# Three dealt schedules in an attention block, and every second scaling of the probabilities on ScalarE

## The chip, the cores and the metric

The kernel runs on one core of one Trainium2 chip. The metric is the time of one execution on the device in microseconds, and its profile is of one such execution.

## The reference

One layer of a hybrid encoder block on x of 1024 tokens by 1024 channels, all in float32:

```
h = RMSNorm(x);  proj = h @ w_in
A: 4 heads, two score maps each; softmax of each, p0 - lam * p1, times v (128 wide)
B: 8 heads of 64, own chunk of 64 and 8 chunks before it, bias by relative place
C: 8 heads of 64, causal, score + c_q - c_k (cumulative log forget)
x += (sum_i sigmoid(gate_i) * (o_i @ w_br_i)) @ w_out
x += (silu(RMSNorm(x) @ w_gate) * (RMSNorm(x) @ w_up)) @ w_down;  out = RMSNorm(x)
```

## The kernel before, in words

Every product is done in three passes of TensorE on a high and a low part of each operand (`three_passes`, L183 to L185). The kernel has four blocks: norm, attention, merge, feed-forward. Only the attention block is touched. It begins near 80 us and ends near 829 us.

**Units.** The attention block goes through 12 units, four for each branch: units 0 to 3 are A (one head of two maps), 4 to 7 B (two heads), 8 to 11 C (two heads). A unit has 16 steps, s = 0 to 15: a step is one tile of 128 queries of one map or head against its keys. The number of key tiles n grows with s, to 8 in A and C and to 5 in B. In B and C steps 0 to 15 have n = 1, 2, 1, 2, 3, 4, 3, 4 and then 5, 5, ... (B) or 5, 6, 5, 6, 7, 8, 7, 8 (C).

**One step's way through the engines**, with the short names used below:
- S(s): TensorE, scores of step s into PSUM (`score`, L930, L931; in C also the causal mask, L933).
- READ(s): VectorE adds the bias, takes the row's extreme and writes to SBUF (`read_scores`, L781); in C it also makes the shift (L790).
- exp(s): ScalarE, in place, with the row sum (`exp`, L652).
- SCALE(s), in B and C: VectorE takes the reciprocal of the row sum (L812) and multiplies the row by it in place (`scale_probs`, L814). In A it is MIX(i) for two steps at once: reciprocal, ratio, and p0 - lam * p1 (`mix_maps`, L822 to L827).
- T(s): TensorE transposes the row by tiles into the turn banks 4 and 5 (`turn_probs`, L959); in A only for odd s. A row of more than 4 tiles takes two chunks, and a chunk has to wait until the bank of the chunk two before it has been read.
- CHhi(s), CHlo(s): ScalarE copies a chunk out (L665, L667), then VectorE makes its low part (L799, L802).
- V(g): TensorE multiplies by v, once for every two steps (`times_v_a` L975, L977; `times_v_bc` L993, L994); then o_low on ScalarE (L676, L684) and o_out on VectorE (L838, L848). V(g) waits for o_out(g-1).

**Projection in between.** TensorE also projects k, q and v of the next unit: 24 pieces of 6 matmuls, in 6 groups of 4. Four pieces stand ahead of the steps, and `PIECES_AT[s]` says how many follow T(s). `EVAC_AT` says in which step a group is taken out of PSUM: `project_out` on ScalarE (L627 to L633) and, for groups 0 to 3, `project_low` on VectorE (two instructions of one group, L743 to L752). `SPLIT_AT` says in which step ScalarE makes the high part of the next weight slab (`split_hi`, L618, called SPLIT below); GpSimd then makes the low part (L591, POOL split). A group may start once the group before it in the same PSUM bank is out (`PROJ_BANKS`); groups 1, 3, 4 and 5 share bank 6. Unit 11 has nothing after it but two groups of a gate, and a list of its own, `LAST_PIECES_AT`.

**Order.** Each engine has its own instruction stream, written as a loop over s, and all of them run in order. In iteration s, which goes from 0 to 17, the order before is:
- TensorE: S(s+2), T(s), pieces, and V(s/2-1) when s is even.
- ScalarE: project_out, CHhi(s), exp(s+2), SPLIT, and o_low when s is odd.
- VectorE, A: MIX (s even), project_low, READ(s+2), CHlo(s), o_out (s odd). B and C: project_low, READ(s+2), SCALE(s+1), CHlo(s), o_out (s odd).

Of the kernel before, what the change touches and what calls it, by code (L numbers as in the profile page):

```python
# [32 lines left out]
P = 128  # L33
# [81 lines left out]

PIECES_AT = [2, 2, 2, 2, 1, 1, 1, 1, 0, 1, 1, 1, 1, 1, 1, 2, 0]
EVAC_AT = {0: 0, 2: 1, 4: 2, 8: 3, 13: 4, 16: 5}
SPLIT_AT = {0: 1, 4: 2, 8: 3}
PROJ_BANKS = (3, 6, 1, 6, 6, 6)
LAST_PIECES_AT = [0, 1, 0, 1, 0, 1, 0, 1, 0, 1, 0, 1, 0, 1, 1, 0, 0]  # L120
LAST_EVAC_AT = {8: 0, 16: 1}
assert sum(LAST_PIECES_AT) == 2 * GROUP_PIECES
assert PIECES_BEFORE + sum(PIECES_AT) == 6 * GROUP_PIECES

# [293 lines left out]
def block_attention(nc, ps, keep, scratch, w_in_k, w_br_b):  # L418
    h_hi, h_lo, ident = keep["h_hi"], keep["h_lo"], keep["ident_r"][:, :].bitcast(F32)
    with ExitStack() as ctx:  # L420
# [35 lines left out]
        probs_ready, rinv_ready, ratio_ready, mixed = sem("probs_ready"), sem("rinv_ready"), sem("ratio_ready"), sem("maps_mixed")  # L456
        scaled = sem("probs_scaled")
        turned, turned_hi, turned_out = sem("chunk_turned"), sem("chunk_hi"), sem("chunk_out")
# [155 lines left out]
        def _(act):  # L614
# [30 lines left out]
            def exp(b, c, s):  # L645
# [3 lines left out]
                else:  # L649
# [4 lines left out]
                                     accum_out=rowsum[:, s % 4:s % 4 + 1]).then_inc(probs_ready, 1)  # L654

            def chunks_hi(b, c, s):
                done, tile = chunks_through(b, s - 1), 0
                i, m = place_of(b, s)
                for j, size in enumerate(chunks_of(b, i)):
                    lc = done + j  # L660
                    act.wait_ge(turned, c["banks"] + (V_CHUNKS + lc + 1))
                    if b == 0:
                        if lc >= 4:
                            act.wait_ge(pv_chunk, c["chunks"] + (lc - 3))
                        nc.scalar.activation(pta_hi[:, lc % 4, 0:size * P], turn_bank[lc % 2][:, 0:size * P], ACT.Copy).then_inc(turned_hi, 1)  # L665
                    else:
                        nc.scalar.activation(turned_place(ptb_hi, b, i, m, tile, size),  # L667
                                             turn_bank[lc % 2][:, 0:size * P].rearrange("p (t q) -> p t q", q=P),
                                             ACT.Copy).then_inc(turned_hi, 1)
                    tile += size  # L670
# [15 lines left out]
            def unit_body(b, it, du, last=False):  # L686
# [5 lines left out]
                for lc in range(V_CHUNKS):  # L692
                    v_hi(b, c, lc, du)
                for s in range(STEPS + 2):
                    if last and s in LAST_EVAC_AT:
                        project_out(UNITS, LAST_EVAC_AT[s], 0)
                    elif not last and s in EVAC_AT:
                        project_out(c["unit"] + 1, EVAC_AT[s], 1 - du)
                    if s in turns:
                        chunks_hi(b, c, s)  # L700
                    if s + 2 < STEPS:
                        exp(b, c, s + 2)
                    if last and s == 3:
                        act.wait_ge(w_loaded[1], 8 * LAST_SLAB + 24)
                        nc.scalar.activation(w_hi[:, 1, 0:BR_K, :], w_raw[:, 1, 0:BR_K, :], ACT.Copy).then_inc(w_hi_done, 1)
                    if not last and s in SPLIT_AT:
                        j = SPLIT_AT[s]
                        odd = 3 * (du + 1) + j
                        act.wait_ge(proj_ready, 2 * (slab + (j - 1)))
                        split_hi(slab + j, odd % 2, 6 * b + 3 * it + odd // 2)  # L710
                    if b == 0 and s >= 3 and s % 2 == 1:
                        o_low_a(c, (s - 3) // 2)
                    if b > 0 and s >= 3 and s % 2 == 1:
                        o_low_bc(c, (s - 3) // 2)

# [20 lines left out]
        def _(dve):  # L736
# [71 lines left out]
            def scale_probs(b, c, s):  # L808
# [3 lines left out]
                nc.vector.reciprocal(rinv[:, s % 4:s % 4 + 1], rowsum[:, s % 4:s % 4 + 1]).then_inc(rinv_ready, 1)  # L812
                dve.wait_ge(rinv_ready, UPB * UNIT_OUTS + turns)
                nc.vector.tensor_scalar(row, row, rinv[:, s % 4:s % 4 + 1], None, ALU.mult).then_inc(scaled, 1)  # L814

# [35 lines left out]
            def unit_body(b, it, du, project=True):  # L851
# [12 lines left out]
                if b > 0:  # L864
                    scale_probs(b, c, 0)
                for s in range(STEPS + 2):
                    if b == 0 and s % 2 == 0 and s < STEPS:
                        mix_maps(c, s // 2)
                    if project and s in EVAC_AT:
                        project_low(c["unit"] + 1, EVAC_AT[s], 1 - du)  # L870
                    if s + 2 < STEPS:
                        read_scores(b, c, s + 2)
                    if b > 0 and s + 1 < STEPS:
                        scale_probs(b, c, s + 1)
                    if s in turns:
                        chunks_low(b, c, s)
                    if b == 0 and s >= 3 and s % 2 == 1:
                        o_out_a(c, (s - 3) // 2)
                    if b > 0 and s >= 3 and s % 2 == 1:
                        o_out_bc(c, (s - 3) // 2)  # L880

# [14 lines left out]
        def _(pe):  # L896
# [48 lines left out]
            def turn_probs(b, c, s):  # L945
# [5 lines left out]
                else:  # L951
                    pe.wait_ge(scaled, STEPS * (c["unit"] - UPB) + (s + 1))
                    src = probs_of(b, s)
# [43 lines left out]
            def unit_body(b, it, du, last=False):  # L997
                c = counts(b, it, du) | {"par": du}
                turns = turns_of(b)
                pieces_at = LAST_PIECES_AT if last else PIECES_AT  # L1000

# [848 lines left out]
```

## Time and profile before

| | us |
|---|---|
| median of 3 runs | 2068.73 (2067.91 to 2071.92) |
| the profiled execution | 2067.87 |
| its span, first to last instruction | 2066.1 |
| TensorE busy | 1962.2 |
| VectorE, ScalarE, GpSimd busy | 1030.5, 703.9, 95.0 |
| mean granted TensorE clock | 0.992 |

The three other blocks keep TensorE almost without a gap; the attention block takes about 36% of the span and has nearly all the gaps that are left. One unit of A takes 60.3 us, one of B 61.4 us, one of C 68.8 us. A time behind the name of an engine is what it is busy; a time in square brackets behind an instruction is how long its engine stood idle ahead of it, with the instruction that released it.

### The profile page before, as it was taken

To read this page: it belongs to the slowest core of one execution; us is meant where nothing else is said; L and a number is where in the kernel's file an instruction comes from. 1 tells how busy PE (TensorE), PEld (TensorE's weight loads), DVE (VectorE), ACT (ScalarE), POOL (GpSimd) and SP (SyncE) were. 2 spreads that over 40 slices of the span, in tenths; PEclk is the share of its full clock that TensorE was granted. 3 is DMA by queue.
4 is the path that set the end of the run, shared out by engine and by line. 5 is a ranking of instruction groups with operands and counts; after the bars stand their busy time and mean duration, and the time that the engine had idled before them with its cause. 6 is when DMAs were issued, how large, how long until landed. Compare 5 with 4: busy or idle time off the path is not lost. (4 is left out here: it accounts for less than half of the span.)

```text
span 2066.1 us, 26269 instructions
## 1 busy us (share of the span) xinstructions
PE 1962.2 (95%) x9542; PEld 1629.9 (79%) x9542; DVE 1030.5 (50%) x1950; ACT 703.9 (34%) x1310; POOL 95.0 (5%) x59
## 2 busy tenths in 40 slices
PE   6999999999999998999999999999999999999997
PEld 3777778878778777788787878788888888888886
DVE  4466666666777787324433237623343334323326
ACT  5355555555555555221431112421112101121122
POOL 1111111110110000000000000000000000000000
PEclk9999999999999999999999999999999999999998
DMA  7422222212222110412111123120121101211112
GB/s 227 124 62 64 69 74 64 65 50 75 51 82 72 42 47 31 123 46 82 51 46 46 46 89 111 30 68 25 51 61 52 49 30 51 61 51 41 41 51 82
DMA packets 145268, 133.32 MB, mean 65 GB/s; under 512 B 7476, under 2 KB 130484, under 8 KB 142888
## 3 DMA queue, kind: packets, MB, share of 16 engines
q1 hardware_dynamic: 141768, 132.16, 21.6%
q8 instruction: 44, 0.72, 0.1%
q10 hardware_dynamic: 3424, 0.17, 0.1%
q14 instruction: 32, 0.26, 0.0%
HBM read 109.17 MB, written 16.06 MB: 61 GB/s over the span
## 5 line engine op out<-in xcount | busy, mean ns | idle before, releaser
L183 PE MATMUL ps<-h_hi,w_hi 128*128 128x512 f32 x1664 | 667.1, 401 | 13.5 <-DVE w_lo L1223 4.7
L185 PE MATMUL ps<-h_hi,w_lo 128*128 128x512 f32 x1664 | 651.7, 392 | 0.0
L184 PE MATMUL ps<-h_lo,w_hi 128*128 128x512 f32 x1664 | 651.3, 391 | 0.0
L183 PEld LDWEIGHTS ps<-h_hi,w_hi 128*128 128x128 f32 x1664 | 314.2, 189 | 77.4 <-DVE w_lo L1223 4.8
L185 PEld LDWEIGHTS ps<-h_hi,w_lo 128*128 128x128 f32 x1664 | 313.7, 189 | 67.4
L184 PEld LDWEIGHTS ps<-h_lo,w_hi 128*128 128x128 f32 x1664 | 314.6, 189 | 59.0
L1598 DVE TENSOR_TENSOR residual<-residual,ps 128x512 f32<-128x512 f32 x240 | 162.7, 686 | 113.7 <-PE ps L185 109.0
L1589 DVE TENSOR_TENSOR w_lo<-w_raw,w_hi 128x1024 fp32r<-128x1024 f32 x46 | 56.4, 1226 | 158.5 <-ACT w_hi L1491 158.5
L1499 ACT ACTIVATE bias<-ps 128x512 f32<-128x512 f32 x44 | 26.1, 594 | 311.5 <-PE ps L185 311.5
L184 PE MATMUL ps<-w_down_lo,act_hi 128*128 128x512 f32 x320 | 124.6, 389 | 0.0
L185 PE MATMUL ps<-w_down_hi,act_lo 128*128 128x512 f32 x320 | 124.6, 389 | 0.0
L183 PE MATMUL ps<-w_down_hi,act_hi 128*128 128x512 f32 x320 | 124.6, 389 | 0.0
L959 PE MATMUL ps<-ident_r,probs_bc 128*128 128x128 f32 x528 | 82.5, 280 | 37.4 <-DVE probs_tb_lo L802 26.1
L667 ACT ACTIVATE probs_tb_hi<-ps 128x384 fp32r<-128x384 f32 (+2 forms) x192 | 81.8, 461 | 103.2 <-PE ps L959 102.5
L591 POOL TENSOR_TENSOR w_lo<-w_raw,w_hi 128x1024 fp32r<-128x1024 f32 (+1 forms) x36 | 85.7, 2381 | 634.3 <-ACT w_hi L618 594.1
L1607 DVE TENSOR_TENSOR bias<-ps,bias 128x512 f32<-128x512 f32 x44 | 30.4, 692 | 167.2 <-PE ps L185 167.2
L781 DVE CUSTOM_DVE_ANT_0 probs_bc<-ps,bias 128x640 f32<-128x640 f32 (+7 forms) x128 | 90.2, 705 | 41.8 <-PE ps L931 15.8
L802 DVE TENSOR_TENSOR probs_tb_lo<-ps,probs_tb_hi 128x384 fp32r<-128x384 f32 (+2 forms) x192 | 93.9, 517 | 17.6 <-ACT probs_tb_hi L667 17.3
L959 PEld LDWEIGHTS ps<-ident_r,probs_bc 128*128 128x128 f32 x528 | 58.7, 141 | 53.1 <-DVE probs_bc L814 29.4
L814 DVE TENSOR_SCALAR probs_bc<-probs_bc,rinv 128x640 f32<-128x640 f32 (+7 forms) x128 | 95.2, 744 | 4.6
L930 PE MATMUL ps<-k_stack,q_stack 128*128 128x320 f32 (+5 forms) x288 | 97.0, 341 | 0.0
L1504 ACT ACTIVATE act_hi<-bias 128x512 fp32r<-128x512 f32 x44 | 27.8, 632 | 202.9 <-DVE bias L1607 202.9
(202 smaller groups left out, 2740.8 us busy)
## 6 DMA issues: line engine op xcount, KB each, us to landing
w_raw<-in_w_in SPq DMA_DIRECT2D x60, 512.0 KB, 3.8
w_raw<-in_w_gate_up SPq DMA_DIRECT2D x44, 512.0 KB, 3.8
k_stack<-k_stack SPq DMA_DIRECT2D x24, 512.0 KB, 6.3
w_raw<-in_w_down SPq DMA_DIRECT2D x22, 512.0 KB, 3.5
x_all<-in_x SPq DMA_DIRECT2D x8, 512.0 KB, 8.6
bias<-bias_a_scratch SPq DMA_DIRECT2D x4, 1024.0 KB, 6.0
heads_bc_scratch<-heads_out SPq DMA_DIRECT2D x8, 512.0 KB, 2.9
bias<-neg_c_scratch SPq DMA_DIRECT2D x4, 1024.0 KB, 5.1
```

The lines of the kernel that those rows point to most:

```text
L183: nc.tensor.matmul(out, w_hi, x_hi, start=first, stop=False)
L184: nc.tensor.matmul(out, w_hi, x_lo, start=False, stop=False)
L185: return nc.tensor.matmul(out, w_lo, x_hi, start=False, stop=last)
L591: nc.gpsimd.tensor_tensor(w_lo[part], w_raw[part], w_hi[part].bitcast(F32), ALU.subtract).then_inc(w_split, 1)
L667: nc.scalar.activation(turned_place(ptb_hi, b, i, m, tile, size), turn_bank[lc % 2][:, 0:size * P].rearrange("p (t q) -> p t q", q=P), ACT ...
L781: nc.vector.tensor_tensor_reduce(out=row_view(probs_of(b, s)[:, 0:n * P], n), in0=scores_view(s, n), in1=row_view(window, n), scale=-1.0, ...
L802: nc.vector.tensor_tensor(turned_place(ptb_lo, b, i, m, tile, size), turn_bank[lc % 2][:, 0:size * P].rearrange("p (t q) -> p t q", q=P), ...
L814: nc.vector.tensor_scalar(row, row, rinv[:, s % 4:s % 4 + 1], None, ALU.mult).then_inc(scaled, 1)
L930: nc.tensor.matmul(dst, q, k_st[:, par, 2 * m, keys], start=True, stop=False)
L959: last = nc.tensor.transpose(turn_bank[lc % 2][:, x * P:(x + 1) * P], src[:, tile * P:(tile + 1) * P], ident[:, :])
L1589: nc.vector.tensor_tensor(w_lo[kind], w_raw[:, raw, :], w_hi[kind].bitcast(F32), ALU.subtract).then_inc(w_split, 1)
L1598: nc.vector.tensor_tensor(res[:, t, cols], res[:, t, cols], bank(ps, 4 + o % 4), ALU.add).then_inc(added, 1)
```

## The change

Four things, all in the attention block:
1. `PIECES_AT`, `EVAC_AT` and `SPLIT_AT` get a list for each branch. The number of pieces for a unit is the same. A moves one piece from step 9 to 10; B and C are dealt anew, in the late steps mostly two in an odd iteration and none in an even one. Evacuations move with the groups; SPLITs move to iterations 0, 2, 10 (A), 0, 3, 12 (B), and stay at 0, 4, 8 in C.
2. In B and C the multiplication of SCALE(s) for even s goes to ScalarE as an activation (Copy with a scale from SBUF, `scale_probs` of ScalarE). The reciprocal stays on VectorE for all s.
3. ScalarE's order in an iteration becomes: project_out, SPLIT, o_low, CHhi(s), the scaling of s+1 (s odd), exp(s+2).
4. VectorE's order in A becomes: READ(s+2), MIX, CHlo(s), project_low, o_out. B and C keep theirs.

```diff
+PIECES_AT = [
+    [2, 2, 2, 2, 1, 1, 1, 1, 0, 0, 2, 1, 1, 1, 1, 2, 0],
+    [3, 2, 1, 1, 1, 2, 0, 1, 1, 2, 0, 1, 1, 2, 0, 2, 0],
+    [2, 1, 2, 2, 1, 2, 2, 1, 1, 1, 0, 1, 0, 2, 0, 2, 0],
+]
+EVAC_AT = [
+    {0: 0, 2: 1, 4: 2, 8: 3, 13: 4, 16: 5},
+    {1: 0, 2: 1, 5: 2, 9: 3, 13: 4, 16: 5},
+    {1: 0, 3: 1, 5: 2, 7: 3, 12: 4, 16: 5},
+]
+SPLIT_AT = [{0: 1, 2: 2, 10: 3}, {0: 1, 3: 2, 12: 3}, {0: 1, 4: 2, 8: 3}]
...
-        scaled = sem("probs_scaled")
+        scaled = [sem("probs_scaled_even"), sem("probs_scaled_odd")]
...
+            def scale_probs(b, c, s):
+                row = probs_of(b, s)[:, 0:tiles_of(b, place_of(b, s)[0])[1] * P]
+                act.wait_ge(rinv_ready, UPB * UNIT_OUTS + STEPS * (c["unit"] - UPB) + (s + 1))
+                nc.scalar.activation(row, row, ACT.Copy, scale=rinv[:, s % 4:s % 4 + 1]).then_inc(scaled[0], 1)
...
+                if b > 0:
+                    scale_probs(b, c, 0)
                 for s in range(STEPS + 2):
...
-                    if s in turns:
-                        chunks_hi(b, c, s)
-                    if s + 2 < STEPS:
-                        exp(b, c, s + 2)
...
-                    if b == 0 and s >= 3 and s % 2 == 1:
-                        o_low_a(c, (s - 3) // 2)
-                    if b > 0 and s >= 3 and s % 2 == 1:
-                        o_low_bc(c, (s - 3) // 2)
+                    if s >= 3 and s % 2 == 1:
+                        if b == 0:
+                            o_low_a(c, (s - 3) // 2)
+                        else:
+                            o_low_bc(c, (s - 3) // 2)
+                    if s in turns:
+                        chunks_hi(b, c, s)
+                    if b > 0 and s % 2 == 1 and s + 1 < STEPS:
+                        scale_probs(b, c, s + 1)
+                    if s + 2 < STEPS:
+                        exp(b, c, s + 2)
...
-                dve.wait_ge(rinv_ready, UPB * UNIT_OUTS + turns)
-                nc.vector.tensor_scalar(row, row, rinv[:, s % 4:s % 4 + 1], None, ALU.mult).then_inc(scaled, 1)
+                if s % 2 == 1:
+                    dve.wait_ge(rinv_ready, UPB * UNIT_OUTS + turns)
+                    nc.vector.tensor_scalar(row, row, rinv[:, s % 4:s % 4 + 1], None, ALU.mult).then_inc(scaled[1], 1)
...
+                    if b > 0 and project and s in EVAC_AT[b]:
+                        project_low(c["unit"] + 1, EVAC_AT[b][s], 1 - du)
+                    if s + 2 < STEPS:
+                        read_scores(b, c, s + 2)
                     if b == 0 and s % 2 == 0 and s < STEPS:
                         mix_maps(c, s // 2)
-                    if project and s in EVAC_AT:
-                        project_low(c["unit"] + 1, EVAC_AT[s], 1 - du)
-                    if s + 2 < STEPS:
-                        read_scores(b, c, s + 2)
                     if b > 0 and s + 1 < STEPS:
                         scale_probs(b, c, s + 1)
                     if s in turns:
                         chunks_low(b, c, s)
...
+                    if b == 0 and s in EVAC_AT[b]:
+                        project_low(c["unit"] + 1, EVAC_AT[b][s], 1 - du)
...
-                    pe.wait_ge(scaled, STEPS * (c["unit"] - UPB) + (s + 1))
+                    pe.wait_ge(scaled[s % 2], STEPS // 2 * (c["unit"] - UPB) + (s // 2 + 1))
```

## Rows read from the trace of the kernel before

**Rows 1.** The page, part 1: busy time and share of the span.
```profile
PE 1962.2 (95%) x9542; PEld 1629.9 (79%) x9542; DVE 1030.5 (50%) x1950; ACT 703.9 (34%) x1310; POOL 95.0 (5%) x59
```
**Rows 2.** Stretches: length, then busy us (and instructions) by engine, clock, DMA.
```profile
85.47:145.75 60.28, 56.63 (x309) 47.95 (x308) 37.94 (x86) 30.02 (x67) 7.34 (x4) 1.00 0.21 52
326.54:387.94 61.40, 57.60 (x333) 49.36 (x332) 43.08 (x106) 34.28 (x79) 7.77 (x5) 1.00 0.24 65
641.74:710.51 68.77, 62.97 (x369) 54.23 (x368) 52.71 (x122) 37.10 (x79) 7.17 (x3) 1.00 0.22 62
776.76:830.00 53.24, 42.99 (x268) 36.79 (x267) 41.49 (x115) 30.18 (x69) 1.27 (x1) 0.97 0.08 30
744.00:748.00 4.00, 1.92 (x13) 1.66 (x12) 3.86 (x12) 2.78 (x7) 0.71 (x1) 0.97 0.00 0
748.00:752.00 4.00, 4.00 (x16) 3.44 (x16) 3.90 (x6) 1.77 (x5) 1.68 (x1) 0.60 0.27 57
```
**Rows 3.** Groups of instructions by shape, 325 to 822 us: busy, mean ns, idle before.
```profile
L959 PE MATMUL ps<-ident_r,probs_bc 128*128 128x128 f32 x520 | 81.5, 280 | 37.4 <-DVE probs_tb_lo L802 26.1 <-DVE probs_bc L814 11.1
...
L814 DVE TENSOR_SCALAR probs_bc<-probs_bc,rinv 128x128 f32<-128x128 f32 x16 | 18.6, 1160 | 0.6
...
L652 ACT ACTIVATE probs_bc<-probs_bc,neg_max 128x640 f32<-128x640 f32 x32 | 26.6, 831 | 6.9 <-DVE neg_max L781 6.8
...
L652 ACT ACTIVATE probs_bc<-probs_bc,shift 128x1024 f32<-128x1024 f32 x8 | 9.2, 1153 | 1.6 <-DVE shift L790 1.4
...
L652 ACT ACTIVATE probs_bc<-probs_bc,shift 128x128 f32<-128x128 f32 x8 | 3.2, 401 | 8.1 <-DVE shift L790 8.1
...
L705 ACT ACTIVATE w_hi<-w_raw 128x512 fp32r<-128x512 f32 x1 | 0.6, 615 | 0.0
```
**Rows 4.** Instructions in order of time, unit 2 (branch A): start us, us, engine.
```profile
214.00 2.39 POOL L591 TENSOR_TENSOR w_lo<-w_raw,w_hi 128x1024 fp32r<-128x1024 f32 x1 [31.69 <-ACT w_hi L618]
...
215.19 1.48 DVE L827 SCALAR_TENSOR_TENSOR probs_a<-probs_a,ratio 128x256 f32<-128x256 f32 x1
...
233.56 0.35 ACT L676 ACTIVATE o_low<-ps,rinv 128x128 f32<-128x128 f32 x1
...
234.43 0.38 PE L975 MATMUL ps<-v_split,probs_ta_hi 128*128 128x256 f32 x1 [0.78 <-DVE heads_out L838]
...
234.72 0.89 DVE L827 SCALAR_TENSOR_TENSOR probs_a<-probs_a,ratio 128x640 f32<-128x640 f32 x1
...
236.33 0.69 DVE L752 SCALAR_TENSOR_TENSOR q_stack<-ps,q_stack 64x512 fp32r<-64x512 f32 x1
237.05 0.96 DVE L781 CUSTOM_DVE_ANT_0 probs_a<-ps,bias 128x768 f32<-128x768 f32 x1
...
242.51 0.38 PE L975 MATMUL ps<-v_split,probs_ta_hi 128*128 128x256 f32 x1 [1.61 <-DVE heads_out L838]
```
**Rows 5.** In order of time, unit 4 (branch B), iterations 9 and 10.
```profile
357.50 0.31 PE L930 MATMUL ps<-k_stack,q_stack 128*128 128x320 f32 x1
357.65 0.31 PE L931 MATMUL ps<-k_stack,q_stack 128*128 128x320 f32 x1
...
359.75 0.77 PE L959 MATMUL ps<-ident_r,probs_bc 128*128 128x128 f32 x5 [1.79 <-DVE probs_tb_lo L802]
...
360.61 2.39 POOL L591 TENSOR_TENSOR w_lo<-w_raw,w_hi 128x1024 fp32r<-128x1024 f32 x1 [9.41 <-ACT w_hi L618]
...
360.88 2.48 DVE L814 TENSOR_SCALAR probs_bc<-probs_bc,rinv 128x640 f32<-128x640 f32 x1
...
363.87 0.77 PE L959 MATMUL ps<-ident_r,probs_bc 128*128 128x128 f32 x5 [1.39 <-DVE probs_tb_lo L802]
...
365.58 0.55 DVE L814 TENSOR_SCALAR probs_bc<-probs_bc,rinv 128x640 f32<-128x640 f32 x1
```
**Rows 6.** In order of time, unit 8 (branch C), iterations 5 and 6.
```profile
664.45 2.35 DVE L814 TENSOR_SCALAR probs_bc<-probs_bc,rinv 128x384 f32<-128x384 f32 x1
...
666.85 0.55 PE L959 MATMUL ps<-ident_r,probs_bc 128*128 128x128 f32 x3 [1.13 <-DVE probs_bc L814]
```

More of the change, by code:

```diff
@@ L114 @@
 PIECES_BEFORE_V = 2
-PIECES_AT = [2, 2, 2, 2, 1, 1, 1, 1, 0, 1, 1, 1, 1, 1, 1, 2, 0]
-EVAC_AT = {0: 0, 2: 1, 4: 2, 8: 3, 13: 4, 16: 5}
-SPLIT_AT = {0: 1, 4: 2, 8: 3}
+PIECES_AT = [
[3 rows of a table added]
+]
+EVAC_AT = [
[3 rows of a table added]
+]
+SPLIT_AT = [{0: 1, 2: 2, 10: 3}, {0: 1, 3: 2, 12: 3}, {0: 1, 4: 2, 8: 3}]
 PROJ_BANKS = (3, 6, 1, 6, 6, 6)
@@ L122 @@
 assert sum(LAST_PIECES_AT) == 2 * GROUP_PIECES
-assert PIECES_BEFORE + sum(PIECES_AT) == 6 * GROUP_PIECES
+assert all(PIECES_BEFORE + sum(pieces) == 6 * GROUP_PIECES for pieces in PIECES_AT)
 def counts(b, it, du):
@@ L696, in unit_body @@
                         project_out(UNITS, LAST_EVAC_AT[s], 0)
-                    elif not last and s in EVAC_AT:
-                        project_out(c["unit"] + 1, EVAC_AT[s], 1 - du)
-                    if s in turns:
-                        chunks_hi(b, c, s)
-                    if s + 2 < STEPS:
-                        exp(b, c, s + 2)
+                    elif not last and s in EVAC_AT[b]:
+                        project_out(c["unit"] + 1, EVAC_AT[b][s], 1 - du)
                     if last and s == 3:
@@ L705, in unit_body @@
                         nc.scalar.activation(w_hi[:, 1, 0:BR_K, :], w_raw[:, 1, 0:BR_K, :], ACT.Copy).then_inc(w_hi_done, 1)
-                    if not last and s in SPLIT_AT:
-                        j = SPLIT_AT[s]
+                    if not last and s in SPLIT_AT[b]:
+                        j = SPLIT_AT[b][s]
                         odd = 3 * (du + 1) + j
@@ L876, in unit_body @@
                         chunks_low(b, c, s)
[L877 to L880, printed above, removed]
+                    if b == 0 and s in EVAC_AT[b]:
+                        project_low(c["unit"] + 1, EVAC_AT[b][s], 1 - du)
+                    if s >= 3 and s % 2 == 1:
+                        if b == 0:
+                            o_out_a(c, (s - 3) // 2)
+                        else:
+                            o_out_bc(c, (s - 3) // 2)
             for g in range(4):
@@ L999, in unit_body @@
                 turns = turns_of(b)
-                pieces_at = LAST_PIECES_AT if last else PIECES_AT
+                pieces_at = LAST_PIECES_AT if last else PIECES_AT[b]
                 done = [0]
```

## The prediction

> **What bounds the kernel now.** The page first: TensorE is busy 95% of the span [rows 1], so only its gaps, its clock and its work can give time, and the change leaves its work as it is. Then the stretches, to see where the gaps lie. One unit of A has 60.28 - 56.63 = 3.65 us of gaps, one of B 3.80, one of C 5.80, and the last unit with its end 10.25 [rows 2]. VectorE is busy 63%, 70% and 77% of these units, ScalarE 50 to 56%: neither is full, so the gaps are moments in which one of them comes late. Then the groups: TensorE's transposes T wait 37.4 us in B and C, 26.1 for CHlo and 11.1 for SCALE, both on VectorE [rows 3]. Last the instructions in order of time, to see why VectorE was late. Three causes come back in every unit:
> - In A, V waits 0.78 and 1.61 us for o_out, which waits for an o_low that stands behind CHhi and exp on ScalarE [rows 4]. Both follow an iteration in which ScalarE had waited for a READ that stood behind MIX and project_low.
> - In B and C, two project_low instructions of 0.69 us each stand ahead of READ and CHlo in iteration 8; T(9) waits 1.79 us for CHlo in B [rows 5].
> - A SCALE of 640 columns takes 0.55 us, but 2.48 us beside a POOL split of 2.39 us, and T(10) behind it waits 1.39 us [rows 5]. In C a SCALE of 384 takes 2.35 us, and T(6) waits 1.13 us [rows 6]. The mean of the 128-column form, 1160 ns, is such a mixture [rows 3].
>
> What a gap costs is a little more than its idle time: matmuls of 320 columns start 0.15 us apart and show as 0.31 us [rows 5], so about 0.16 us is hidden at each. With five to seven stops a unit the losses are about 4.4 us (A), 4.7 (B), 7.0 (C). C loses clock too: behind the stretch with TensorE busy 1.92 of 4 us the granted clock is 0.60 for 4 us, a mixture of 1.2 and 2.4 GHz, and costs 4 x 0.4 = 1.6 us [rows 2].
>
> **The scaling moved.** For B and C, 8 units, 64 scalings go from VectorE to ScalarE. ScalarE has no such operation yet. From below, a plain copy takes 0.615 us for 512 columns; from above, exp takes 0.401, 0.831 and 1.153 us for 128, 640 and 1024 [rows 3]. I take exp, since it also reads a value per partition, and drop its sum read-out: 0.40, 0.62, 0.83 and 1.04 us for 1, 3, 5 and 7 tiles, by its line. That is 5.4 us in a unit of B, 5.8 in C, 44.6 in all; 0.1 us less for each by the copy, 38. VectorE loses, at its free speed (0.55 us for 640 columns, so about 0.47 on the mean of these sizes, an estimate), some 30 us. Worth more: the long SCALEs are those of steps 2 and 10 (B) and 2, 6, 10 (C), all even, so this class of waits leaves VectorE: some 2 us each, 17 of them, 33 us. Not all was on the path: that of step 2 made TensorE wait for nothing.
>
> The page of the Trainium skill "Perfetto Trace Analysis", section "Optimizing Scalar/DVE Operations", speaks against the move: where VectorE has its faster mode it is the quicker engine, and work should leave it only when it is full. It is not full here [rows 2]. By that rule the 64 moves add 44.6 - 30 = 14.6 us of work; were all of it on the path, the 40 us summed below would be 25, and the time 2044. It is a form of the first rival below.
>
> Where is ScalarE's new work hidden? It stands in odd iterations ahead of exp(s+2). Late in B and C those now mostly hold two pieces (2 x 1.4 us), so from T(s) to T(s+1) there are 3.8 us, in which CHhi (about 0.8), the scaling 0.83 and exp 0.83 + 0.19 fit. exp(s+2) comes some 0.8 us later; behind it stand CHhi(s+1) and SCALE(s+2), with an even iteration's V to cover them. In C at iterations 10 to 12, with 0, 1 and 0 pieces, VectorE's and TensorE's work are level (3.4 against 3.1 us in iteration 12); I count 0.4 us there. If this cover is gone, each scaling costs up to its own length.
>
> **The deal of pieces and evacuations, B and C.** I followed the queues with the durations above. B: group 3 ends in iteration 8, is taken out in 9, and the next piece stands in 9: one project_out (about 0.6 us, as the copy of 512 columns [rows 3]), two project_low of 0.69 [rows 4] and the semaphores between end 2.55 us after the group, while V, S and T cover 2.1: 0.45 us. C: the same in iteration 7, 0.2, and T(8) behind it 0.3. The SPLIT ahead of exp at iteration 4 of C lets the POOL split start before SCALE(5): blocked 2 us, of which T(5) sees 0.4. Iteration 0 of both meets SCALE(1) in the same way, hidden behind three pieces in B, 0.1 us in C. In B SPLIT in 3 and 12 misses the scalings. New waits: B 0.6, with 0.6 more for what I didn't find, C 1.4. Kept of the loss: B 4.7 - 1.2 = 3.5 gained, 14 for four units (unit 6 has one wait more); C 7.0 - 1.4 = 5.6 for three units, 17, with the clock loss of unit 9 within it.
>
> **A.** READ ahead of MIX and project_low lets exp start 1 to 2 us sooner, o_low is first in its iteration, SPLIT moves to iteration 2 where ScalarE waits anyway. All of 4.4 us would go. Two waits come. In iterations 8 and 9 there are no pieces: from S(10), READ(10) starts after 1.07 us, takes 0.9 to the next start, reciprocal and ratio 0.42 and MIX(4) 0.89 [rows 4], 3.3 us in all, while S, V and S take TensorE 2.5: T(9) waits 0.8. SPLIT at 10 ends about 7.9 us after S(10), and MIX(5) wants to start at 8.2: a MIX beside a POOL split was stretched to 1.48 us, to the split's end [rows 4], so T(11) comes 1.4 us late. Should MIX start first, this is nothing. 4.4 - 2.2 = 2.2 us a unit, 9 for four; 3.6 a unit at best.
>
> The SPLIT in A, B and C moves ahead of CHhi and exp by at most 1.1 us, and the DMA of the slab after it moves with it; the slab is needed only many pieces later, and no TensorE wait for a load shows in the attention block. Reordering o_low costs CHhi 0.36 us, covered as above.
>
> **Unit 11** keeps its list. It lives from VectorE, 78% busy [rows 2], and ScalarE's added 5.8 us is in the same chain as VectorE's 3.9 less. I take nothing, from +3 to -3.
>
> **Sum.** 9 + 14 + 17 + 0 = 40 us of the profiled 2067.87. The followed queues hold only the waits I looked for; I take off 0.5 us for each of the 11 full units: 34.5. The median shown is 0.9 above the profiled one. 2068.7 - 34.5 = 2034.
>
> **Rivals.**
> - *The waits move* (0.17): T waits for the scaling on ScalarE or for MIX beside the split in most units, and half the 40 us comes back. For it: the evacuations fit by tenths of a microsecond, and ScalarE's copies of T's output come within each iteration. Against it: the free time of both engines [rows 2]. About 2049.
> - *ScalarE becomes the late link* (0.09), the other side: each scaling delays exp(s+2), that READ's successor and the next odd SCALE by its full length, and no piece covers it. Then 44.6 us stand against 40: 2073. It decides from 0.63 us exposed at each of the 64. Against it: ScalarE is 54% busy in C, about 65% after.
> - *Nothing* (0.06): the relief and the added work cancel, 2068.
> - *All gaps go* (0.13), with no MIX beside the split and no clock loss: A 3.6 x 4, B 4.2 x 4, C 6.8 x 3 with unit 11 giving 3: 54 us, 2015.
> - The forecast has 0.55, its own range 2024 to 2044.
>
> **Numbers.** 0.2% is 4 us, about what a measurement here can tell. Faster: 0.55 + 0.17 + 0.13 and a little of the rest, 0.87; same 0.05; slower 0.08. The range goes from the best case to beyond half the gain: 2014 to 2056.
>
> **What would show it.** L814 x64 with no form near 1160 ns; 64 new ScalarE copies of 0.4 to 1.05 us; V's 0.78 and 1.61 us waits in A gone; a wait of T for MIX in iterations 9 and 11 of A; units of about 58, 58 and 63 us; clock 1.00 from 740 to 760 us. I am wrong if T's wait is for the new ScalarE copies by over 0.6 us a time, or if A's units don't shorten.

## The result, and the profile after

The changed kernel takes 2018.38 us (2015.51 to 2020.33, 4 runs), the kernel before 2068.77: ratio 0.9753, 95% interval 0.9736 to 0.9769. That is 50.4 us faster; 34.5 were forecast. The time lies in the stated range of 2014 to 2056, but outside the 2024 to 2044 of the forecast itself; it is nearest to the rival *all gaps go* (2015, chance 0.13). The profiled execution is the fastest of the four: 2015.51 us, with a span of 2013.7 against 2066.1. Below, times of stretches are of that execution. Line numbers differ after the change: S is L952 and L953, READ L799, exp L660, MIX L846, VectorE's SCALE L833, ScalarE's scaling L667, T L981, CHhi L678 and L680, V L997 and L1015, SPLIT L626, POOL split L599, o_low L689 and L697, o_out L857 and L867.

The page, part 1, to be read beside [rows 1]:

```profile
PE 1947.1 (97%) x9542; PEld 1626.9 (81%) x9542; DVE 982.1 (49%) x1886; ACT 747.6 (37%) x1374; POOL 95.4 (5%) x59
```

The number of matmuls is the same. VectorE has 64 instructions fewer and is busy 48 us less, ScalarE has 64 more and is busy 44 us more.

Stretches of one unit of A, B, C, and of the last unit to beyond its end, as in [rows 2]:

```profile
144.31:202.07 57.76, 55.52 (x310) 47.91 (x309) 38.00 (x86) 32.85 (x68) 7.41 (x4) 1.00 0.26 73
317.59:374.18 56.59, 56.56 (x334) 49.50 (x332) 37.23 (x98) 38.98 (x87) 7.84 (x5) 1.00 0.26 70
545.04:607.49 62.45, 61.92 (x369) 54.28 (x368) 45.99 (x114) 41.98 (x87) 7.19 (x3) 1.00 0.24 69
729.57:780.00 50.43, 40.14 (x268) 35.66 (x267) 38.12 (x108) 36.01 (x80) 1.29 (x1) 1.00 0.13 46
```

The gaps of TensorE went from 3.65 to 2.24 us in A, from 3.80 to 0.03 in B, from 5.80 to 0.53 in C. By unit starts (the first transpose of v): A 10.0 us shorter in four units, B 19.0, the first three units of C 19.3, the last unit to the end of its last o_out 5.2 (52.6 to 47.4, with its clock at 1.00 where it was 0.97), together 53.5. What stands ahead of unit 0 is 1.1 us longer, which makes the 52.4 of the spans; its code is the same, and its length goes from 85.3 to 87.8 us in the traces below. The section on the time before says that the attention block has nearly all the gaps: by the trace of before it has 56.6 of 103.9 us. The rest, 16.8 us ahead of the block and 30.5 behind it, the change doesn't touch. Where the clock had fallen in the middle of C, it now holds:

```profile
740.00:760.00 20.00, 19.70 (x131) 17.73 (x130) 18.76 (x53) 17.19 (x38) 0.61 (x1) 1.00 0.00 1
```

Groups by shape, 317 to 780 us, as in [rows 3]:

```profile
L981 PE MATMUL ps<-ident_r,probs_bc 128*128 128x128 f32 x528 | 80.7, 276 | 6.6 <-ACT probs_bc L667 5.3 <-DVE probs_bc L833 1.1 <-DVE probs_tb_lo L820 0.2
...
L667 ACT ACTIVATE probs_bc<-probs_bc,rinv 128x640 f32<-128x640 f32 x24 | 20.0, 832 | 4.7 <-DVE rinv L830 4.4
L833 DVE TENSOR_SCALAR probs_bc<-probs_bc,rinv 128x256 f32<-128x256 f32 x16 | 15.7, 981 | 0.6
...
L667 ACT ACTIVATE probs_bc<-probs_bc,rinv 128x384 f32<-128x384 f32 x16 | 9.9, 617 | 9.2 <-DVE rinv L830 9.1
...
L667 ACT ACTIVATE probs_bc<-probs_bc,rinv 128x896 f32<-128x896 f32 x8 | 8.4, 1045 | 2.1 <-DVE rinv L830 1.7
...
L667 ACT ACTIVATE probs_bc<-probs_bc,rinv 128x128 f32<-128x128 f32 x16 | 6.4, 403 | 11.9 <-DVE rinv L830 11.4
```

T waited 37.4 us, and now 6.6. The copy on ScalarE costs what exp costs in [rows 3] (832 ns for 640 columns against 831). And the blocked SCALEs (held up by a POOL split on GpSimd) aren't gone: the mean of the 256-column form is 981 ns, where an unblocked one took 353. 17 SCALEs took over 1 us before, 9 do now.

Unit 2 (A) in order of time, the two waits that were forecast to come:

```profile
231.39 0.76 PE L981 MATMUL ps<-ident_r,probs_a 128*128 128x128 f32 x5 [0.90 <-DVE probs_a L846]
...
235.92 2.39 POOL L599 TENSOR_TENSOR w_lo<-w_raw,w_hi 128x1024 fp32r<-128x1024 f32 x1 [19.13 <-ACT w_hi L626]
...
236.24 2.88 DVE L846 SCALAR_TENSOR_TENSOR probs_a<-probs_a,ratio 128x768 f32<-128x768 f32 x1
...
239.18 0.87 PE L981 MATMUL ps<-ident_r,probs_a 128*128 128x128 f32 x6 [1.34 <-DVE probs_a L846]
```

Unit 8 (C), iteration 4, a SCALE of an odd step that the POOL split holds up, as SCALE(6) was in [rows 6]. TensorE waits 0.20 us for it, where it waited 1.13 for SCALE(6):

```profile
562.23 2.39 POOL L599 TENSOR_TENSOR w_lo<-w_raw,w_hi 128x1024 fp32r<-128x1024 f32 x1 [10.64 <-ACT w_hi L626]
...
563.07 1.84 DVE L833 TENSOR_SCALAR probs_bc<-probs_bc,rinv 128x512 f32<-128x512 f32 x1
...
564.96 0.66 PE L981 MATMUL ps<-ident_r,probs_bc 128*128 128x128 f32 x4 [0.20 <-DVE probs_bc L833]
```

### The profile page after: what moved, and what is told of

The parts are those of the page before. It is cut to its first block and busy times, and to the rows that moved or that the text cites. A ratio compares the mean times of both kernels' runs of the same rounds, so it can differ in the third digit from the quotient of the medians.

```text
span 2013.7 us, 26237 instructions
## 1 busy us (share of the span) xinstructions
PE 1947.1 (97%) x9542; PEld 1626.9 (81%) x9542; DVE 982.1 (49%) x1886; ACT 747.6 (37%) x1374; POOL 95.4 (5%) x59
## 5 line engine op out<-in xcount | busy, mean ns | idle before, releaser
L191 PEld LDWEIGHTS ps<-h_hi,w_hi 128*128 128x128 f32 x1664 | 313.8, 189 | 73.3 <-DVE w_lo L1245 4.8
L799 DVE CUSTOM_DVE_ANT_0 probs_bc<-ps,bias 128x640 f32<-128x640 f32 (+7 forms) x128 | 90.4, 707 | 55.8 <-PE ps L953 28.2
L599 POOL TENSOR_TENSOR w_lo<-w_raw,w_hi 128x1024 fp32r<-128x1024 f32 (+1 forms) x36 | 86.1, 2392 | 582.2 <-ACT w_hi L626 522.9
L820 DVE TENSOR_TENSOR probs_tb_lo<-ps,probs_tb_hi 128x384 fp32r<-128x384 f32 (+2 forms) x192 | 93.5, 514 | 15.7 <-ACT probs_tb_hi L680 14.9
L680 ACT ACTIVATE probs_tb_hi<-ps 128x384 fp32r<-128x384 f32 (+2 forms) x192 | 81.9, 461 | 47.3 <-PE ps L981 45.1
L952 PE MATMUL ps<-k_stack,q_stack 128*128 128x320 f32 (+5 forms) x288 | 96.8, 340 | 0.0
L953 PE MATMUL ps<-k_stack,q_stack 128*128 128x320 f32 (+5 forms) x288 | 94.7, 332 | 0.0
L1211 ACT ACTIVATE gate_sigmoid<-ps 128x512 f32<-128x512 f32 x46 | 27.4, 598 | 169.3 <-PE ps L193 169.2
L981 PE MATMUL ps<-ident_r,probs_bc 128*128 128x128 f32 x528 | 80.7, 276 | 6.6 <-ACT probs_bc L667 5.3
```

The costliest lines, as they stand in the source:

```text
L191: nc.tensor.matmul(out, w_hi, x_hi, start=first, stop=False)
L599: nc.gpsimd.tensor_tensor(w_lo[part], w_raw[part], w_hi[part].bitcast(F32), ALU.subtract).then_inc(w_split, 1)
L799: nc.vector.tensor_tensor_reduce(out=row_view(probs_of(b, s)[:, 0:n * P], n), in0=scores_view(s, n), in1=row_view(window, n), scale=-1.0, ...
L820: nc.vector.tensor_tensor(turned_place(ptb_lo, b, i, m, tile, size), turn_bank[lc % 2][:, 0:size * P].rearrange("p (t q) -> p t q", q=P), ...
L952: nc.tensor.matmul(dst, q, k_st[:, par, 2 * m, keys], start=True, stop=False)
L953: last_one = nc.tensor.matmul(dst, q, k_st[:, par, 2 * m + 1, keys], start=False, stop=not diagonal)
```

## The experiments

The change has three parts: the lists, the orders (ScalarE's, and VectorE's in A), and the scaling on ScalarE. Six kernels take the combinations that the two traces leave open; the other six vary one thing in the changed kernel or go on from it. Where an edit is long, the fence tells it in words.

### The orders alone

```diff
 # the kernel before, and:
+ ScalarE: project_out, SPLIT, o_low, CHhi(s), exp(s+2)
+ VectorE, A: READ(s+2), MIX, CHlo(s), project_low, o_out
```

> The kernel before with only the new orders of ScalarE and of VectorE in A; old lists, every scaling on VectorE. My theory (three causes of their own: order, lists, blocked scalings): A falls from 60.3 to about 58.0 us a unit, since its two waits for o_out go; B and C keep the blocked SCALEs and the late evacuation and give at most 1 us a unit. In all 10 to 14 us, about 2057. Rival (the moved scaling gives nearly everything in B and C and the order nothing outside A): the same A, B and C unchanged, 2059. Second rival (the order alone does it): B near 58, C near 65, about 2030.

Measured: 2084.18 us, ratio 1.0072 (1.0056 to 1.0089): slower by less than a percent, but clear of the noise. A did more than was expected, 60.3 to 57.1 us a unit. B and C got much longer, which no theory had. The second unit of each:

```profile
380.50:447.64 67.14, 59.78 (x333) 51.82 (x332) 43.47 (x102) 33.48 (x75) 7.49 (x5) 0.95 0.21 58
653.86:725.51 71.65, 63.94 (x369) 55.47 (x368) 51.51 (x122) 37.78 (x79) 7.06 (x3) 0.98 0.20 59
```

Unit 5 (B), iterations 8 and 9, in order of time. L632 and L633 are project_out, L755 and L758 project_low, L618 SPLIT, L591 the POOL split, L787 READ, L820 SCALE, L808 CHlo, L968 T:

```profile
413.20 0.59 ACT L633 ACTIVATE q_stack<-ps 64x512 fp32r<-64x512 f32 x1
...
413.81 1.06 ACT L618 ACTIVATE w_hi<-w_raw 128x1024 fp32r<-128x1024 f32 x1
...
414.05 0.69 DVE L758 SCALAR_TENSOR_TENSOR q_stack<-ps,q_stack 64x512 fp32r<-64x512 f32 x1
...
414.90 0.77 ACT L672 ACTIVATE probs_tb_hi<-ps 128x384 fp32r<-128x384 f32 x2
...
415.02 2.35 POOL L591 TENSOR_TENSOR w_lo<-w_raw,w_hi 128x1024 fp32r<-128x1024 f32 x1 [10.53 <-ACT w_hi L618]
...
415.72 2.00 DVE L820 TENSOR_SCALAR probs_bc<-probs_bc,rinv 128x640 f32<-128x640 f32 x1
...
417.64 0.87 DVE L808 TENSOR_TENSOR probs_tb_lo<-ps,probs_tb_hi 128x384 fp32r<-128x384 f32 x2
...
418.24 1.12 PE L968 MATMUL ps<-ident_r,probs_bc 128*128 128x128 f32 x4 [3.07 <-DVE probs_tb_lo L808]
```

In the old lists groups 2 and 3 are evacuated in iterations 4 and 8, and SPLITs 2 and 3 stand in the same two. With SPLIT ahead of CHhi and exp, the copy of T's output stands behind 1.2 us of project_out and 1.06 of SPLIT, the POOL split starts while VectorE still works off project_low and READ, and SCALE(9) then meets it. T(9) pays for all of it, for iteration 8 has no piece. T(5) waits 2.20 us for SCALE(5) in the same way, and T(1) 1.79 us for SCALE(1). These stops are not all of the loss: the unit is 5.7 us longer than one of before, its gaps are 3.6 us longer, and its matmuls are busy 2.2 us longer at a granted clock of 0.95.

### The moved scaling alone

```diff
 # the kernel before, and for even s in B and C:
+ ScalarE: project_out, CHhi(s), Copy(s+1) by rinv (s odd), exp(s+2), SPLIT, o_low
```

> The kernel before with only the scalings of even steps on ScalarE, ahead of exp(s+2); old lists, old orders. My theory: the waits behind a SCALE beside a POOL split go (1.4 us in B, 1.1 and 1.0 in C), the waits for the late evacuation stay: B 61.4 to about 59.5, C 68.8 to about 66, A unchanged; about 2051. Rival (the moved scaling gives nearly all of B and C): B 57, C 63, about 2030. Rival of the other side (ScalarE late without the new order): B and C longer than before.

Measured: 2067.15 us, ratio 0.9991 (0.9981 to 1.0001): nothing to be told. B 60.2, C 66.5 (a second one 68.1), the last unit 56.3 against 52.6. Not one SCALE of VectorE took over 1 us, so the cause was removed as meant. B and C gave 1.2 and 2.3 us a unit where the clock held. In units 6 and 9 it was 0.97 for 1.00 before; unit 6 was 0.6 us longer than before, and unit 9 only 0.7 shorter. V waits for o_out in B (0.75 us a unit) and C (1.01), and in the last unit at six places; four of them:

```profile
784.46 0.38 PE L1005 MATMUL ps<-probs_tb_hi,v_split 128*128 128x256 f32 x1 [1.40 <-DVE heads_out L859]
...
789.50 0.39 PE L1005 MATMUL ps<-probs_tb_hi,v_split 128*128 128x256 f32 x1 [0.63 <-DVE heads_out L859]
...
795.62 0.38 PE L1005 MATMUL ps<-probs_tb_hi,v_split 128*128 128x256 f32 x1 [1.01 <-DVE heads_out L859]
...
809.64 0.39 PE L1005 MATMUL ps<-probs_tb_hi,v_split 128*128 128x256 f32 x1 [0.94 <-DVE heads_out L859]
```

o_low stands behind the scaling and exp in the old order, and V behind o_low. Here "Perfetto Trace Analysis" of the Trainium skill, in "Optimizing Scalar/DVE Operations", would have been right: VectorE was not full, and the work taken from it bought nothing.

### The lists alone

```diff
 # the kernel before, with PIECES_AT, EVAC_AT and SPLIT_AT of the changed kernel
```

> The kernel before with only the lists for each branch; old orders, every scaling on VectorE. My theory: evacuation of group 3 one step later in B and earlier in C, two pieces in odd iterations: B about 59, C about 66.5, A unchanged or longer by the SPLIT at 10 that meets MIX(5); about 2050. Rival (lists matter only with the rest): within 5 us of before, since SCALEs are still blocked by the splits at their new places.

Measured: 2037.12 us, ratio 0.9852 (0.9832 to 0.9872), 31.6 us of the 50. One unit of each branch:

```profile
144.67:204.07 59.40, 56.34 (x310) 47.99 (x308) 37.96 (x86) 31.39 (x68) 7.39 (x4) 1.00 0.26 71
322.81:380.94 58.13, 57.20 (x334) 49.49 (x333) 40.09 (x106) 34.55 (x79) 7.58 (x5) 1.00 0.25 68
556.54:620.23 63.69, 62.70 (x370) 54.27 (x368) 47.98 (x122) 37.34 (x79) 7.21 (x3) 1.00 0.23 67
```

My theory had B and C right in kind and about 1 and 3 us too long, and A, which was to stay or to get longer, is 0.9 us shorter. The rival (within 5 us of before) fell. T(9)'s wait for the late evacuation in B, 1.79 us before, is 1.80 with the scaling alone and 3.07 with the orders alone; here it is gone, so it was the lists that took it away. Its row with the scaling alone:

```profile
360.57 0.77 PE L971 MATMUL ps<-ident_r,probs_bc 128*128 128x128 f32 x5 [1.80 <-DVE probs_tb_lo L812]
```

The SCALEs over 1 us fell from 17, of up to 2.48 us, to 7 of at most 1.51, with every scaling still on VectorE. In C the SPLITs keep their iterations, so there the pieces and the evacuations alone give 5.1 us a unit.

### The whole without the moved scaling

```diff
 # the changed kernel, and for even s too:
+ VectorE: tensor_scalar(row, row, rinv, mult); no scaling on ScalarE
```

> The changed kernel with every scaling back on VectorE (lists and orders new). It prices the move of the scaling within the whole. My theory: A stays at 57.8; in B the splits at 3 and 12 start just where no VectorE scaling is due or one that started before, so B loses about 1 us (57.6); C meets two blocked SCALEs and has VectorE and TensorE level late, so it loses 2 to 3 us (65): in all 12 to 15 us over the changed kernel, about 2031. Rival (the Trainium skill, Perfetto Trace Analysis: an engine that is not full should keep what it does faster): the same time or faster than the changed kernel, 2010 to 2018.

Measured: 2030.54 us, ratio 0.982 (0.98 to 0.984). Within the whole the moved scaling is worth 12.2 us: 1.5 a unit in B, 0.8 in C, 5.0 in the last unit (52.3 against 47.4 to its last o_out; the clock there was 0.94 against 1.00, about 3 us of it). The total came out as my theory had it, by other parts: B lost 1.5 for the 1 expected, C 0.8 for 2 to 3, and the last unit, of which nothing was said, the rest. The rival (an engine that is not full keeps its work) falls: what held for the scaling alone doesn't hold within the whole.

### The whole without the lists, and without the orders

```diff
 # first: the changed kernel with the lists of before
 # second: the changed kernel with the two orders of before
```

> The changed kernel with the lists of before (orders new, even scalings on ScalarE). With the orders alone B went from 61.4 to 66.6 and C to 72, and every blocked SCALE was that of steps 1, 5 and 9, which are odd and stay on VectorE here. Theory (the new orders put SPLIT ahead of exp, so that the POOL split starts just before the odd SCALE, and the new lists are what takes the splits away from it in B and covers it in C): B stays near 65, C near 70, A at 57.1 as with the orders alone; about 2068. Rival (the moved scaling frees enough of VectorE to make up for it): B near 60, C near 66, about 2035.

> The changed kernel with the orders of before (lists new, even scalings on ScalarE). Lists alone gave A 59.4, B 58.1, C 63.7. Theory (moving the scaling pays only where o_low does not stand behind it): A 59.4, B 57.5, C 63.5, and the last unit longer by its waits of V for o_out, as with the moved scaling alone; about 2036, no better than the lists alone. Rival (each part pays what it pays, whatever the others are): the scaling gives its 12 us on top of the lists, about 2025.

Measured: 2093.5 us, ratio 1.0112 (1.0097 to 1.0128), and 2057.55, ratio 0.9938 (0.9922 to 0.9953). Without the lists B is at 68.2, C at 73.3 and 71.8: slower than expected, and slower than the orders alone. Without the orders B is at 60.1, C at 65.6: the moved scaling makes the lists' kernel 20.4 us slower. The theory for that run expected 2036, no better than the lists alone; a loss of 20 us it had not foreseen. TensorE's waits in the last unit of the second (us in total, times, longest):

```profile
PE ps L1013 <- DVE heads_out L867: 6.6, 6, 1.9
PE ps L979 <- ACT probs_bc L667: 3.8, 2, 3.3
```

All eight, medians in us, then from the traces a unit of A, the second unit of B, the first of C, and the last unit to the end of its last o_out:

| lists | orders | scaling | whole kernel | A | B | C | last unit |
|---|---|---|---|---|---|---|---|
| - | - | - | 2068.8 | 60.3 | 61.4 | 68.8 | 52.6 |
| - | - | new | 2067.2 | 60.3 | 60.2 | 66.5 | 56.3 |
| - | new | - | 2084.2 | 57.1 | 67.1 | 72.9 | 52.3 |
| - | new | new | 2093.5 | 57.1 | 68.2 | 73.3 | 49.9 |
| new | - | - | 2037.1 | 59.4 | 58.1 | 63.7 | 53.6 |
| new | - | new | 2057.6 | 59.4 | 60.1 | 65.6 | 56.0 |
| new | new | - | 2030.5 | 57.8 | 58.1 | 63.2 | 52.3 |
| new | new | new | 2018.4 | 57.8 | 56.6 | 62.5 | 47.4 |

The lists of the branches don't reach the last unit, so its code is the same in pairs of these kernels, and the pairs show what the granted clock does: 52.6 and 53.6 us without the two other parts (clock 0.97 and 0.94), 49.9 and 47.4 with both (0.93 and 1.00). At a clock of 0.93 to 0.94 the last unit takes 53.6 us with neither, 56.0 to 56.3 with the scaling alone, 52.3 with the orders alone and 49.9 with both. Its rows in the kernels with the lists alone, with orders and scaling, and in a kernel further below that has the last unit of the changed one:

```profile
744.79:798.34 53.55, 44.13 (x268) 37.90 (x267) 41.42 (x115) 30.24 (x69) 1.27 (x1) 0.94 0.09 30
804.13:854.01 49.88, 42.74 (x268) 37.88 (x267) 37.61 (x107) 34.40 (x77) 1.30 (x1) 0.93 0.09 33
729.84:780.13 50.29, 43.08 (x268) 38.19 (x267) 37.59 (x107) 34.43 (x77) 1.30 (x1) 0.93 0.09 32
```

So the changed kernel's 47.4 us is that of an execution in which the clock held: the same code with the same gaps of 7.22 us took 50.3 in another, and the profiled execution is 2.9 us faster than the median.

### The other parity

```diff
 # the changed kernel, in B and C:
- ScalarE scales s+1 for s odd, VectorE the odd steps
+ ScalarE scales s+1 for s even, VectorE the even steps
```

> The changed kernel, but ScalarE scales the odd steps (in even iterations) and VectorE the even ones. Theory A (the POOL split meets the odd SCALE of steps 1 and 5, and the even iterations of ScalarE have no o_low): the blocked SCALEs go altogether and the time is the same or a little better, 2012 to 2020. Theory B (cover counts, which the two pieces of the odd iterations give to the even steps alone): T of odd steps follows at 2.5 us on the T before it, and waits for ScalarE's copy of 0.83 us: B and C 2 to 4 us a unit longer, 2030 to 2045.

Measured: 2032.8 us, ratio 0.982 (0.9805 to 0.9835). Both theories were half right. C is better, 62.1 us without any wait. B is worse, 59.6, but not for want of cover on ScalarE: the blocked SCALE is now an even one, in iteration 3, whose SPLIT goes with one piece. With a further wait of 0.75 us of a piece for project_low it makes the 2.4 us of gaps of a unit of B.

```profile
331.67 2.37 POOL L599 TENSOR_TENSOR w_lo<-w_raw,w_hi 128x1024 fp32r<-128x1024 f32 x1 [9.31 <-ACT w_hi L626]
...
331.83 2.43 DVE L831 TENSOR_SCALAR probs_bc<-probs_bc,rinv 128x384 f32<-128x384 f32 x1
...
334.39 0.54 PE L979 MATMUL ps<-ident_r,probs_bc 128*128 128x128 f32 x3 [1.63 <-DVE probs_bc L831]
```

### A mended

```diff
-SPLIT_AT = [{0: 1, 2: 2, 10: 3}, ...
+SPLIT_AT = [{0: 1, 2: 2, 11: 3}, ...
...
+                    if b == 0 and s == 8:
+                        mix_maps(c, s // 2)
                     if s + 2 < STEPS:
                         read_scores(b, c, s + 2)
-                    if b == 0 and s % 2 == 0 and s < STEPS:
+                    if b == 0 and s % 2 == 0 and s < STEPS and s != 8:
                         mix_maps(c, s // 2)
```

> The changed kernel with two edits in A: SPLIT 3 in iteration 11 and not 10, so that the POOL split does not meet MIX(5), and MIX ahead of READ in iteration 8 alone. Theory (the two waits of T for MIX, 0.90 and 1.34 us in each unit of A, come from these two): both go, 57.8 to 55.4 us a unit, 9 to 10 us in all, about 2008. Rival (the time comes back as a wait for o_out or for the evacuation of group 3, since READ(10) is later): less than 4 us gained.

Measured: 2008.12 us, ratio 0.9712 (0.9695 to 0.973). A unit of A takes 55.5 us, and both waits are gone. Of the rival's new wait 0.24 us a unit came (a piece for project_low). The MIX of 768 columns is back at 1.02 us, for it now starts before SPLIT does:

```profile
230.80 1.02 DVE L846 SCALAR_TENSOR_TENSOR probs_a<-probs_a,ratio 128x768 f32<-128x768 f32 x1
...
231.46 1.04 ACT L626 ACTIVATE w_hi<-w_raw 128x1024 fp32r<-128x1024 f32 x1
...
232.64 2.40 POOL L599 TENSOR_TENSOR w_lo<-w_raw,w_hi 128x1024 fp32r<-128x1024 f32 x1 [20.56 <-ACT w_hi L626]
```

### SPLIT put back beside the evacuations in B

```diff
-{0: 1, 3: 2, 12: 3}
+{0: 1, 5: 2, 9: 3}
```

> The changed kernel with one list entry pair moved: in B the SPLITs 2 and 3 stand in iterations 5 and 9, those in which a group is evacuated, and not in 3 and 12. Theory (the new orders are slow where project_out, project_low and SPLIT share an iteration, since READ, CHhi and exp then all stand behind them and the POOL split starts beside the odd SCALE): B goes from 56.6 to 59 to 63 us a unit, with an odd SCALE near 2.4 us and a T waiting behind it; 10 to 25 us in all, A and C unchanged. Rival (pieces and evacuations make the gain of the lists, the place of the SPLIT in B is nothing): within 3 us of the changed kernel.

Measured: 2018.87 us, ratio 0.975 (0.9735 to 0.9765), B at 56.6. The theory fell: project_out, project_low and SPLIT in one iteration cost nothing here.

```profile
337.03 1.06 ACT L626 ACTIVATE w_hi<-w_raw 128x1024 fp32r<-128x1024 f32 x1
...
338.26 2.40 POOL L599 TENSOR_TENSOR w_lo<-w_raw,w_hi 128x1024 fp32r<-128x1024 f32 x1 [13.29 <-ACT w_hi L626]
...
339.02 0.61 ACT L667 ACTIVATE probs_bc<-probs_bc,rinv 128x384 f32<-128x384 f32 x1
```

What differs from the slow case is that iterations 5 and 9 are odd and have two pieces each, while 4 and 8 had one and none; and that the scaling due beside the POOL split is an even one, on ScalarE, where it takes its 0.61 us. Which of the two it is was not taken apart.

### Smaller ones

> The kernel with A mended (2008) and two of the eight gate pieces of the last unit put ahead of its steps, where T(0) waits 3.3 us for the first scaling. Theory: the wait fills with 2.7 us of work, of which at most some tenths are missing later: 2 to 3 us, about 2005.5, and the clock does not fall behind the wait. Rival (the pieces are missing later, where T waits for VectorE): no gain.

> As the run with the last unit filled, but in units 8 to 10 ScalarE scales the odd steps; B and unit 11 keep the even ones. The run with odd steps on ScalarE had units of C at 62.1 with no wait left, against 62.5. Theory: 0.3 us a unit, 1 us in all, hardly to be told from nothing. Rival: a boundary between the two ways costs it back.

Both build on the kernel with A mended. Measured: 2008.33 us, ratio 0.9702 (0.9689 to 0.9715), and 2008.73, 0.9703 (0.969 to 0.9716): neither can be told from the kernel with A mended. In the last unit T waited for scalings twice, 3.3 and 0.5 us; with the pieces moved it waits four times, 3.0 us in total, the longest 1.3. The pieces are missing later, as the rival had it, but T waits there for ScalarE and not for VectorE. At a clock of 1.00 the unit takes 46.3 us against 47.4, too little for the medians to show. With odd steps on ScalarE C takes 62.1 us a unit as expected, 1.0 us in three units.

```diff
+                for k in range(1):
+                    nc.scalar.activation(spare[:, k, :], keep["ident_r"][:, 0:64].bitcast(F32), ACT.Copy, scale=rinv[:, s % 4:s % 4 + 1])
                 nc.scalar.activation(row, row, ACT.Copy, scale=rinv[:, s % 4:s % 4 + 1]).then_inc(scaled[0], 1)
```

> The changed kernel with one more small copy (64 columns, about 0.33 us) on ScalarE ahead of each of its 64 scalings: 21 us of added work. Theory (two pieces in each late odd iteration cover it; where T waits already it is exposed: once a unit in C and thrice in the last unit): 2 to 6 us slower. Rival (ScalarE is the late link now, and each tenth counts): 15 to 21 us slower.

Measured: 2023.0 us, ratio 0.9779 (0.9764 to 0.9794), 4.6 us over the changed kernel. The group of the added copies, and a unit of B and C:

```profile
L669 ACT ACTIVATE spare<-ident_r,rinv 128x64 f32<-128x64 f32 x64 | 22.2, 348 | 28.3 <-DVE rinv L833 27.0
```

```profile
317.78:374.76 56.98, 56.87 (x334) 49.47 (x333) 37.55 (x98) 40.37 (x95) 7.64 (x5) 1.00 0.26 70
546.94:610.66 63.72, 62.29 (x370) 54.37 (x369) 46.63 (x114) 43.57 (x95) 7.19 (x3) 1.00 0.24 67
```

Of 22.2 us added, about a fifth shows in the medians: 0.4 us a unit in B, 1.3 in C. The profiled last unit is 3.5 us longer, but at a clock of 0.91. The cover that the forecast counted on is there, nearly whole in B, and thinner in C.

## Why the prediction was right, and where it was off

The direction and the kind of gain were right, and so was the walk through A. The size was not: 34.5 us were forecast and 50.4 came, so the time lies outside the forecast's own 2024 to 2044. The term that failed is what was taken off in B and C, and the last unit put at nothing. The rival *all gaps go* was nearest in time, and in B (4.7 us a unit for its 4.2), C (6.4 for 6.8) and the last unit; in A it was wrong, where MIX did meet the split (2.5 for 3.6).

- **What bounds the kernel** was read rightly: only TensorE's gaps could give time, and the waits of the three causes named went, the last but for 0.20 us a unit in C.
- **The price of the scaling on ScalarE** (0.40, 0.62, 0.83, 1.04, 44.6 us in all) measured 0.403, 0.617, 0.832 and 1.045, 44.7 us. The bound by exp was the price, that by the plain copy 0.1 us too low.
- **A**: 2.2 us a unit taken, 2.5 measured, with the waits of T(9) and T(11) at 0.90 and 1.34 us for 0.8 and 1.4. Taking both away gave 10.3 us, 8.9 of it in A, where these terms said 8.8.
- **B and C were mis-sized.** 3.5 and 5.6 us a unit less 0.5 were taken, 4.7 and 6.4 measured. Of the new waits (1.2 in B, 1.4 in C) and the 0.5 off, nothing came in B and 0.6 us in C. The wait for the evacuation of group 3 in B (0.45 us), the 0.6 us a unit for what I didn't find, the 0.3 of T(8) and the level stretch of C (0.4) didn't come; in C T waits 0.27 us for ScalarE and 0.20 for SCALE(5). That is 4 x 1.7 + 3 x 1.3 = 10.7 us more than forecast. The 0.16 us hidden at each stop was too little as well: in B four stops went and TensorE's busy time fell by 1.04 us (57.60 to 56.56), 0.26 each; counting five stops where the trace has four made up for it. And the loss of clock was that of unit 10, not 9. With A's 10.0 for 4 x (2.2 - 0.5) = 6.8, the last unit's 5.2 for nothing, and 1.1 lost ahead of unit 0, this makes the 18 us between 34.5 and the 52.4 of the spans.
- **The last unit was wrong as a step**: nothing was taken, 5.2 us came in the profiled execution, beyond the 3 of its bound. The clock at 1.00 for 0.97 is 1.6 us of it, and that part is luck, for the same code also ran at 0.93. At like clocks the pairs above give 3.7 us: scaling alone 2.6 longer, orders alone 1.3 shorter, both together 3.7 shorter. With the scaling alone V waits for o_out six times, 6.3 us in total, and the new orders take away all but the 1.90 us at the end, so o_low ahead of CHhi removes what the scaling adds. That the rest comes since the unit has few pieces, and every tenth off VectorE's queue counts, is argued and not shown.
- **The reason given for the moved scaling was only half of it.** "This class of waits leaves VectorE" holds for the even steps; SPLIT further ahead made odd ones of the blocked SCALEs, 1.84 to 2.17 us, of which T sees 0.2. No form near 1160 ns was forecast; the 256-column form has 981. And the 33 us of blocked time were worth nothing by themselves: with the scaling alone V waited for a late o_low, and the clock fell in two units. I had followed the whole, and had not seen that the parts depend on one another so much: by the parts' own effects on before, -31.6, +15.5 and -1.6, the sum would be -18.
- **The rival on the other side**, ScalarE as the late link, has its like in the kernel without the new orders (20.4 us lost), but there it is o_low that comes late, with V behind it, and not exp. By the run with longer scalings it doesn't happen in the changed kernel. One of the signs of being wrong did show, a wait of T for a scaling on ScalarE of over 0.6 us, but only at the start of units: 3.31 us in the last unit and 0.71 in unit 6. VectorE's first SCALE had cost 3.19 and 0.76 there before, so it says nothing against the move.

The Trainium skill, "SBUF — State Buffer", in "Who interferes with whom", says that an operation of VectorE in a two-port mode, or with two inputs in SBUF, and one of GpSimd that reads SBUF exclude each other for a whole instruction, and that ScalarE isn't part of it. The traces agree: a SCALE started 0.16 us after the POOL split took 2.43 us, MIX beside it 2.88 and ahead of it 1.02, ScalarE's scaling beside it 0.61. An operation of VectorE with one input in PSUM wasn't held up: CHlo of 256 columns took its usual 0.42 us within the split of unit 4 of the changed kernel.

What stays open: whether the pieces or ScalarE's scaling saves B when SPLIT and evacuation share an iteration, and what the lists' 31.6 us are, taken apart into pieces and evacuations (the trace shows the wait for the late evacuation gone and the blocked SCALEs fewer and shorter, but not what each is worth). Why the clock holds in one execution of the same last unit and falls in another is open too.

## What to carry to other kernels

In kernels of several in-order queues, price a change as a whole: here a new order alone lost 15 us, a moved operation alone gave nothing, both together lost 25, and with lists that put independent TensorE work where the other engines are longest they gave 50. When an operation goes to another queue, look at what stands behind it there and is awaited; moving that ahead (o_low) is part of the move. Following the queues for two or three iterations, with durations from the trace, found the two new waits of A to a tenth of a microsecond, and mending them gave 10 us more. In B and C the same walk found waits of which most didn't come, and a reserve was put on top of them: here that was the error, 1.7 and 1.3 us a unit. And before a gain is read off one traced execution, look at the clock of each stretch: the same last unit took 47.4 and 50.3 us.

## What the runs showed of the hardware

A SCALE or a MIX that is caught by a POOL split on GpSimd lasts as if it did its own work after the split. In the traces here it ends behind GpSimd's end by what it takes alone less 0.20 us, wherever in the split it started: SCALEs of 128, 256, 384, 512, 640 and 768 columns take 0.29, 0.35, 0.42, 0.49, 0.55 and 0.62 us alone, and end 0.08, 0.15, 0.22, 0.28, 0.35 and 0.42 us behind it; MIX of 768 columns takes 1.02 alone and ends 0.81 behind. So a SCALE that starts 0.16 us into a split of 2.37 takes 2.43 us, and one that starts 0.84 into one of 2.39 takes 1.84. Not every VectorE instruction is caught: the shift of one column (L808) took its usual 0.27 us 0.28 us into a split of unit 9 of the changed kernel, and CHlo, with one input in PSUM, its usual 0.42.

The granted clock did not follow from the stops alone. It was 1.00 in all full units of the changed kernel, whose longest stop is 1.35 us, and it was 0.95 to 0.97 in the units of B with the orders alone, with stops of 3.1, 2.2 and up to 1.8 us. But before the change units 8 and 9 of C kept 1.00 with stops of 2.1, 1.1 and 1.0 us, and unit 10, which lacks one of the shorter ones, had 0.97. The last unit of the changed kernel, with gaps of 7.22 us each time, had 1.00, 0.96 and 0.93 in three kernels that don't differ in it, and took 47.4, 48.7 and 50.3 us.
